# Who sums which chunks of the first modulation, and when the rotary keys are turned

## The chip, the cores and the metric

The kernel runs on one core of a Trainium2 chip. The metric is the device time of one execution in microseconds; the median of the runs counts. The core has TensorE (matmuls), VectorE, ScalarE, GpSimd and SyncE (SP), which only issues loads; 16 DMA engines serve all queues.

## What is computed

One layer over 256 tokens of width 2048. The part that matters here is its opening:

```python
ada = jnp.dot(jax.nn.silu(c), w_ada) + b_ada          # c is one row of 2048
shift1, scale1, gate1, shift2, scale2, gate2 = jnp.split(ada[:, None, :], 6, axis=-1)
h = layer_norm(x) * (1 + scale1) + shift1
z, xbc, dt_raw, q_a, kv_a, k_r, g_logits = jnp.split(jnp.dot(h, w_in), IN_OFFSETS, axis=-1)
...
q = jnp.dot(rms_norm(q_a, q_norm_w), w_uq)            # attention (MLA), 16 heads
kv = jnp.dot(rms_norm(kv_a, kv_norm_w), w_ukv)
k_pe = apply_rope(k_r, cos, sin)                      # the rotary keys, shared by all heads
```

After it come attention, a state-space branch, gates, an output projection, and a PEER layer that gathers 128 experts for each token. They are not touched by the change.

## The kernel before

The first modulation (`shift1` and `scale1`) is a product of one row with 2048 x 4096 weights, 32 MB. It is cut into four quarters of 1024 output columns (`QUARTERS`), and each quarter into eight chunks of 256 weight rows, 1 MB each: 32 chunks, numbered n = 8q + j. Five buffers in SBUF hold them (`ADA_BUFS`).

- SP loads the chunks in order (`ada1_chunk`, L521 to L531). For n >= 5 it waits until chunk n - 5 has been used, by the counter `ada_used` (VectorE) or `ada_pe_used` (TensorE). Its queue is in order: a wait holds back all that follows, among it the weights of the first projection, two units of 1 MB for each quarter (`load`, L518), and x, which is asked for after chunk 4.
- VectorE sums chunks j = 0 to 6 of a quarter into an accumulator of 128 partitions (`ada1_chunks`, L1548 and L1550): two instructions a chunk. TensorE sums chunk 7 straight into PSUM with 1-column matmuls (`ada1_rest`, L690), then adds the accumulator's sum over partitions (`ada1_sums`, L699), for which it waits for VectorE (`acc_ready`); `acc_summed` tells VectorE that a quarter's row is there.
- `h_quarter` on VectorE (L1564 to L1574) makes scale and shift from PSUM, applies them to a quarter of the turned, normalised x (`xnT`), waits for ScalarE's rounded copy (`h_hi`, L1125), subtracts it (`h_lo`) and makes the low parts of the quarter's two weight units (`wlo`, L1481), of which ScalarE has made the high parts (`whi`, L1064). TensorE then multiplies the two units (`token_unit`, L634 to L636), three matmuls for each product.
- The order on VectorE: quarter 0's chunks; copies of the parameter columns; normalising x; then for each q from 1: chunks 0 to 2 of q, all of `h_quarter(q - 1)`, chunks 3 to 6 of q. On TensorE: the turns of the parameters, which wait for 17 small loads on ScalarE's queue (`params_in`, L674); chunk 7 and sums of quarter 0; the turns of x (L713); then for each quarter its two units, after them chunk 7 and the sums of the next.

Before attention TensorE turns `dk` (dt and rotary key, L751), VectorE rotates the keys (`kpe2`, L1678 to L1684), TensorE turns them (L756), ScalarE copies them (L1168, L1169, `kpe_read`), and only then TensorE enters attention's loop of four rounds (`pe.Fori(0, 4)`). A round opens with two units of the queries (k = 0, 1: channel matmuls and rope columns), then two of keys and values. In a chunk of code after the rotated keys, VectorE computes dt (L1689 to L1700).

Of the kernel before, what the change touches and what calls it, by code (L numbers as in the profile page):

```python
# [17 lines left out]
P = 128  # L18
# [3 lines left out]
DC = D // P  # L22
# [60 lines left out]

QUARTERS, ADA_V, ADA_BUFS = 4, 7, 5

# [45 lines left out]
def build(nc, a, out, stop="all"):  # L131
    ctx = ExitStack()
    with ctx:
# [272 lines left out]
        b_free = sem("b_free")  # L406
# [101 lines left out]
        def _(sp_):  # L508
# [13 lines left out]
            def ada1_chunk(q, j):  # L522
                n = 8 * q + j
                if n >= ADA_BUFS:

                    q0, j0 = divmod(n - ADA_BUFS, 8)
                    if j0 < ADA_V:
                        sp_.wait_ge(ada_used, q0 * ADA_V + j0 + 1)
                    else:
                        sp_.wait_ge(ada_pe_used, q0 * (8 - ADA_V) + j0 - ADA_V + 1)  # L530
                sp_.dma_start(ada1_in(n), a["p_ada1"][ds(n * P, P), :]).then_inc(ada_full[n % ADA_BUFS], 16)  # L531
# [83 lines left out]
        def _(pe):  # L615
# [63 lines left out]

            ada_sum = aux[:, 3, :]  # L680

            def ada1_rest(q):

                for j in range(ADA_V, 8):
                    n = 8 * q + j
                    pe.wait_ge(ada_full[n % ADA_BUFS], 16 * (n // ADA_BUFS + 1))
                    for kc in range(2):
                        for t in range(8):
                            c = t * P
                            last = mm(ada_sum[:, 8 * q + t:8 * q + t + 1],  # L690
                                      ada1_in(n)[:, 2 * W * kc + c:2 * W * kc + c + P],
                                      csil[:, 2 * j + kc:2 * j + kc + 1], start=(j == ADA_V and kc == 0 and t == 0),
                                      stop=False, skip_group_check=True)
                    last.then_inc(ada_pe_used, 1)

            def ada1_sums(q):
                pe.wait_ge(acc_ready, q + 1)
                for t in range(8):
                    last = mm(ada_sum[:, 8 * q + t:8 * q + t + 1], ada1_acc[:, q % 2, t * P:t * P + P],  # L699
                              con[:, C_ONE:C_ONE + 1], start=False, stop=True, skip_group_check=True)  # L700
                last.then_inc(acc_summed, 1)
# [21 lines left out]
            if on("low"):  # L723
# [9 lines left out]

                for q in range(QUARTERS):
                    pe.wait_ge(h_ready, q + 1)
                    for s in range(2):
                        token_unit(U_LOW, 2 * q + s, 0, 0, h_hi, h_lo, 4 * q, DC - 1,
                                   [ps[:, s, b, :] for b in range(BLK)])
                    if q + 1 < QUARTERS:
                        ada1_rest(q + 1)  # L740
                        ada1_sums(q + 1)
# [6 lines left out]
                for k in range(2):  # L748
                    pe.wait_ge(dk_copied, k + 1)
                    for b in range(BLK):  # L750
                        last = nc.tensor.transpose(aux[:, b, 64 * k:64 * k + 64], dk[:, k, b * P:b * P + P],  # L751
                                                   ident[0:64, 0:64])
                    last.then_inc(dk_turned, 1)
                pe.wait_ge(kpe_ready, 1)
                for b in range(BLK):
                    last = nc.tensor.transpose(aux[:, 3, b * P:b * P + P],  # L756
                                               kpe2[:, b, :, :].rearrange("p a b -> p (a b)"), ident)
                last.then_inc(kpe_turned, 1)
            if on("att"):
                pe.wait_ge(cn_split, 2)  # L760
                pe.wait_ge(kpe_read, 1)
                with pe.Fori(0, 4) as i:
                    for k in range(2):
                        if k == 1:
# [4 lines left out]
                                     [(ps[:, 1, k, e * SEQ:e * SEQ + SEQ], e * QH, e == 0) for e in range(2)], used=False)  # L769
                        if k == 0:  # L770

                            pe.wait_ge(b_free, i + 1)
# [4 lines left out]
                        for b in range(BLK):  # L777
                            o = ps[:, 0, 0, b * 256 + k * P:b * 256 + k * P + P]
                            t = slice(b * P, b * P + P)
                            for kc in range(RC):  # L780
                                mm(o, cqT_hi[:, kc, t], rope[0][:, kc], start=(kc == 0), stop=False)
                                mm(o, cqT_lo[:, kc, t], rope[0][:, kc], start=False, stop=False)
                                last = mm(o, cqT_hi[:, kc, t], rope[1][:, kc], start=False, stop=(kc == RC - 1))
                        last.then_inc(pe_used, 1)
                    for k in range(2):

# [685 lines left out]
        def _(dve):  # L1472
# [63 lines left out]
            def ada1_chunks(q, first, end):  # L1536
                if first == 0:
                    dve.wait_ge(acc_summed, q + 1)
                for j in range(first, end):
# [4 lines left out]
                    for kc in range(2):  # L1544
                        k = 2 * j + kc
                        src = tile[:, 2 * W * kc:2 * W * kc + 2 * W]
                        if k == 0:
# [5 lines left out]
                    if j < ADA_V - 1:  # L1553
                        last.then_inc(ada_used, 1)
                        dve.wait_ge(ada_used, q * ADA_V + j + 1)
                    else:
                        last.then_inc(acc_ready, 1)
                        dve.wait_ge(acc_ready, q + 1)
                        dve.sem_inc(ada_used, 1)

            def h_quarter(q):

                dve.wait_ge(acc_summed, q + 3)
                link(V.tensor_tensor(adacol[:, 4 * q:4 * q + 4], aux[:, 3, 8 * q:8 * q + 4],  # L1564
                                     cols[:, PC_ADA + 4 * q:PC_ADA + 4 * q + 4], ALU.add))
                link(V.scalar_tensor_tensor(adacol[:, DC + 4 * q:DC + 4 * q + 4], aux[:, 3, 8 * q + 4:8 * q + 8], 1.0,
                                            cols[:, PC_ADA + DC + 4 * q:PC_ADA + DC + 4 * q + 4], ALU.add, ALU.add))
                dve.wait_ge(xT_ready, q + 1)
                for k in range(4 * q, 4 * q + 4):
                    last = V.tensor_scalar(xnT[:, k, :], xnT[:, k, :], adacol[:, DC + k:DC + k + 1],  # L1570
                                           adacol[:, k:k + 1], ALU.mult, ALU.add)
                    S.step(last) if k % 4 < 3 else last.then_inc(h_full, 1)
                dve.wait_ge(h_hi_ready, q + 1)
                V.tensor_tensor(h_lo[:, 4 * q:4 * q + 4, :], xnT[:, 4 * q:4 * q + 4, :],  # L1574
# [4 lines left out]
            dve.wait_ge(c_ready, 1)  # L1579
            ada1_chunks(0, 0, ADA_V)  # L1580
            dve.wait_ge(rows_turned, 1)
# [6 lines left out]
            for q in range(1, QUARTERS):  # L1588
                ada1_chunks(q, 0, 3)
                h_quarter(q - 1)  # L1590
                ada1_chunks(q, 3, ADA_V)
            h_quarter(QUARTERS - 1)

            V.memset(kpeT[64:P, 0, :], 0.0).then_inc(kpe_zero, 1)
# [683 lines left out]
```

## Time and profile before

| | us |
|---|---|
| median of 3 runs | 2896.03 (2895.16 to 2896.86) |
| profiled execution | 2899.7 |
| its span, first to last instruction | 2898.0 |
| TensorE busy | 2396.8 (83%) |
| VectorE busy | 2106.9 (73%) |
| ScalarE busy | 1002.1 (35%) |
| GpSimd busy | 882.0 (30%) |
| mean granted clock of TensorE | 0.912 |

Busy shares are means over stages that have different limits. The part that the change touches is the first 195 us or so. There VectorE, TensorE and the loads take turns in being last, so the timeline of each engine and the times at which SP issues its loads say more than the shares. PE stands for TensorE, PEld for its weight loads, DVE for VectorE, ACT for ScalarE, SPq for the issues of SP. A long matmul row "x32" holds 16 matmuls of two pieces each.

### The profile page before, as it was taken

Reading aid. Unit: us, or ns where it says so; the run is one execution under the profiler, and the core shown is the slowest. Engines: PE = TensorE matmul, PEld = TensorE weight load, DVE = VectorE, ACT = ScalarE, POOL = GpSimd, SP = SyncE. Lnnn points to the kernel's source line nnn. Section 1 sums busy time; section 2 is a strip of 40 time slices with the busy share of each in tenths; the row PEclk is TensorE's granted clock in tenths of the full one; section 3 lists DMA queues with packets and bytes.
Section 4 is the critical chain, followed back from the end, with each engine's and each line's share of the span. In section 5 each row is a group of like instructions: output and inputs, shape, how many; then the busy total and the mean of one; then the engine's idle time right before and its main releaser. Section 6 shows DMA issues by size and latency. Waiting matters only on the chain.

```text
span 2898.0 us, 38848 instructions
## 1 busy us (share of the span) xinstructions
PE 2396.8 (83%) x14598; PEld 2021.0 (70%) x14598; DVE 2106.9 (73%) x2541; ACT 1002.1 (35%) x1389; POOL 882.0 (30%) x725
## 2 busy tenths in 40 slices
PE   4589999999999999999869866665656669999990
PEld 3589998888888888999759766665655654444440
DVE  7766668777877786444574788888888896665568
ACT  1144442344444444433343222224767660000000
POOL 0000001122222221000100555756656724444343
PEclk9799999999999999999989878877777889999995
DMA  8745658766656555555544799999999949999995
GB/s 342 294 169 202 223 203 285 254 210 211 204 190 211 197 203 175 221 188 181 210 145 175 279 366 398 372 377 382 375 376 390 394 176 413 413 414 414 415 412 229
DMA packets 144961, 817.83 MB, mean 282 GB/s; under 512 B 16520, under 2 KB 21248, under 8 KB 70832
## 3 DMA queue, kind: packets, MB, share of 16 engines
q0 software_dynamic: 93200, 477.21, 42.4%
q1 hardware_dynamic: 49728, 336.05, 31.4%
q10 hardware_dynamic: 1888, 2.59, 0.2%
q8 instruction: 97, 1.59, 0.2%
q14 instruction: 48, 0.39, 0.0%
HBM read 811.55 MB, written 4.23 MB: 281 GB/s over the span
## 4 chain that ended last, share of the span: by engine, by line
PE 41%; DVE 23%; DMA 21%; issue 8%; POOL 3%; ACT 3%; ACTq 0%; DVEq 0%; POOLq 0%
DMA vrow<-in_p_vg,acc 12%; PE ps L654 9%; PE ps L656 9%; PE ps L655 9%; DMA rrow<-in_peer_u,acc 7%; DVE rrow L2030 4%; DVE ps L2059 3%; POOL rrow L2198 3%; DVE wlo L1481 2%; DVE acc L1530 2%; ACT whi L1064 2%; PE ps L634 2%; PE ps L635 2%; PE ps L636 2%; DVE oh L2072 1%
## 5 line engine op out<-in xcount | busy, mean ns | idle before, releaser
L1481 DVE TENSOR_TENSOR wlo<-raw,whi 128x2048 fp32r<-128x2048 f32 x216 | 504.8, 2339 | 376.6 <-ACT whi L1064 366.6
L1064 ACT ACTIVATE whi<-raw 128x2048 fp32r<-128x2048 f32 x216 | 412.8, 1913 | 707.1 <-PE ps L656 486.2
L2198 POOL DMA_INDIRECT rrow<-in_peer_u,acc x256 | 443.5, 1733 | 455.8 <-DVE acc L1978 202.3
L2030 DVE CUSTOM_DVE_ANT_0 rrow<-rrow,h 128x2048 f32<-128x2048 f32 x200 | 450.0, 2290 | 61.1 <-DMA rrow<-in_peer_u,acc 60.8
L654 PE MATMUL ps<-h_hi,whi 128*128 128x256 f32 (+1 forms) x1568 | 454.9, 290 | 9.3 <-issue 5.7
L2059 DVE SCALAR_TENSOR_TENSOR ps<-vrow,acc,ps 128x1024 f32<-128x1024 f32 x254 | 327.2, 1288 | 167.8 <-DMA vrow<-in_p_vg,acc 154.1
L1049 PE MATMUL aux<-vden,wt 128*128 128x512 f32 x1024 | 441.7, 594 | 4.7 <-DMA vden<-in_p_vd 4.0
L655 PE MATMUL ps<-h_lo,whi 128*128 128x256 f32 (+1 forms) x1568 | 445.1, 284 | 0.0
L656 PE MATMUL ps<-h_hi,wlo 128*128 128x256 f32 (+1 forms) x1568 | 445.0, 284 | 0.0
L1049 PEld LDWEIGHTS aux<-vden,wt 128*128 128x128 f32 x1024 | 195.0, 191 | 250.8 <-issue 245.1
L2198 POOL DMA_INDIRECT vrow<-in_p_vg,acc x256 | 247.4, 966 | 305.6 <-DVE ps L2059 220.0
L654 PEld LDWEIGHTS ps<-h_hi,whi 128*128 128x128 f32 (+1 forms) x1568 | 300.7, 192 | 22.0 <-issue 14.0
L655 PEld LDWEIGHTS ps<-h_lo,whi 128*128 128x128 f32 (+1 forms) x1568 | 300.9, 192 | 4.0 <-issue 3.8
L656 PEld LDWEIGHTS ps<-h_hi,wlo 128*128 128x128 f32 (+1 forms) x1568 | 300.7, 192 | 0.0
L2128 POOL DMA_DIRECT2D ada_in<-in_p_ada x128 | 69.3, 542 | 751.1 <-DVEq L1631 602.1
L994 PE MATMUL ps<-con,rrow 128*128 128x128 f32 x896 | 174.1, 375 | 142.5 <-DMA rrow<-in_peer_u,acc 141.6
L994 PEld LDWEIGHTS ps<-con,rrow 128*128 128x128 f32 x896 | 157.5, 200 | 151.6 <-DMA rrow<-in_peer_u,acc 150.4
L1004 PE MATMUL aux<-hT,rT 128*128 128x128 f32 x1792 | 229.8, 290 | 5.3 <-ACT rT L1382 5.2
L1004 PEld LDWEIGHTS aux<-hT,rT 128*128 128x128 f32 x1792 | 226.4, 208 | 9.4 <-ACT rT L1382 8.8
L1530 DVE SCALAR_TENSOR_TENSOR acc<-ada_in,csil,acc 128x512 f32<-128x512 f32 x240 | 202.3, 843 | 28.5 <-DMA ada_in<-in_p_ada 15.2
L1382 ACT ACTIVATE rT<-ps 128x1024 f32<-128x1024 f32 x112 | 113.0, 1023 | 289.8 <-PE ps L994 289.7
L1079 ACT ACTIVATE st<-st,con 128x2 f32<-128x2 f32 (+1 forms) x18 | 5.2, 294 | 507.6 <-DVE st L1508 507.3
(331 smaller groups left out, 4165.6 us busy)
## 6 DMA issues: line engine op xcount, KB each, us to landing
raw<-in_p_in SPq DMA_DIRECT2D x104, 1024.0 KB, 4.9
ada_in<-in_p_ada POOLq DMA_DIRECT2D x128, 512.0 KB, 5.2
vden<-in_p_vd SPq DMA_DIRECT2D x64, 1024.0 KB, 8.0
ada_in<-in_p_ada SPq DMA_DIRECT2D x32, 1024.0 KB, 9.7
raw<-in_p_so SPq DMA_DIRECT2D x32, 1024.0 KB, 4.8
raw<-in_p_mo SPq DMA_DIRECT2D x16, 1024.0 KB, 7.1
raw<-in_p_bc SPq DMA_DIRECT2D x16, 1024.0 KB, 4.9
raw<-in_p_mix SPq DMA_DIRECT2D x16, 1024.0 KB, 4.8
```

The lines of the kernel that those rows point to most:

```text
L654: mm(o, wh, x_hi[:, k, :], start=(k == 0 and first), stop=False, skip_group_check=True)
L655: mm(o, wh, x_lo[:, k, :], start=False, stop=False, skip_group_check=True)
L656: last = mm(o, wl, x_hi[:, k, :], start=False, stop=(k == klast), skip_group_check=True)
L994: last = nc.tensor.transpose(ps[:, half, t // 4, (t % 4) * P:(t % 4) * P + P], rrow[:, r % ROWS, c:c + P], ident)
L1004: last = mm(aux[:, 3, j * P:j * P + P], rT[:, kc, :], hT[b][:, kc, :], start=(kc == 0), stop=(kc == DC - 1), skip_group_check=True)
L1049: last = mm(aux[:, 2 * b + n, :], wt[b][:, 2 * u + q, :], vden[u % 4][:, q, n * W:n * W + W], start=(u == 0 and q == 0), stop=(u == NVU - ...
L1064: F(whi[:, n % 2, :, 0:cols_], raw[:, n % 4, :, 0:cols_], ACT.Copy).then_inc(hi_ready, 1)
L1481: V.tensor_tensor(wlo[:, n % 2, :, 0:cols_], raw[:, n % 4, :, 0:cols_], whi[:, n % 2, :, 0:cols_].bitcast(F32), ALU.subtract).then_inc(lo_ ...
L1530: last = V.scalar_tensor_tensor(acc_, tile[:, kc, :], csil[:, k:k + 1], acc_, ALU.mult, ALU.add)
L2030: last = V.tensor_tensor_reduce(row, row, h2[:, b, :], 1.0, 0.0, ALU.mult, ALU.add, dots[:, k, e:e + 1])
L2059: last = V.scalar_tensor_tensor(o, row, w, o, ALU.mult, ALU.add)
L2198: return G.indirect_dma_start(out=dst, out_offset=None, in_=table, in_offset=bass.IndirectOffsetOnAxis(ap=eid_all[:, r:r + 1], axis=0))
```

## The change

Four things are changed.

1. VectorE sums six chunks of a quarter instead of seven (`ADA_V` 7 to 6), TensorE two (`ADA_PE`): chunks 0 and 1 instead of chunk 7. SP's waits follow: before chunk n is loaded, n - 5 with j of 0 or 1 must have been used by TensorE, the others by VectorE. This holds for quarter 0 too.
2. On TensorE `ada1_rest(q + 1)` stands ahead of the wait for `h_ready` and of quarter q's units, instead of behind them. The sums of odd quarters go to another PSUM bank, `aux[:, 2]`.
3. On VectorE `h_quarter` is cut in two. Its second part, `h_low`, stands one chunk later: chunk 2 of q, `h_quarter(q - 1)`, chunk 3, `h_low(q - 1)`, chunks 4 to 7.
4. The turn of the rotary keys becomes `turn_kpe`, called behind the first unit (i = 0, k = 0) of attention; the waits for `cn_split` 2, `kpe_read` and (for i = 0) `b_free` move behind the second unit. TensorE's loop over the four rounds is written out (`for i in range(4)`), the other engines keep theirs.

```diff
-QUARTERS, ADA_V, ADA_BUFS = 4, 7, 5
+QUARTERS, ADA_V, ADA_BUFS = 4, 6, 5
+ADA_PE = 8 - ADA_V
...
-                    if j0 < ADA_V:
-                        sp_.wait_ge(ada_used, q0 * ADA_V + j0 + 1)
+                    if j0 < ADA_PE:
+                        sp_.wait_ge(ada_pe_used, q0 * ADA_PE + j0 + 1)
                     else:
-                        sp_.wait_ge(ada_pe_used, q0 * (8 - ADA_V) + j0 - ADA_V + 1)
+                        sp_.wait_ge(ada_used, q0 * ADA_V + j0 - ADA_PE + 1)
...
-            ada_sum = aux[:, 3, :]
+            def ada_sum(q):
+
+                return aux[:, 3 - q % 2, :]
...
-                for j in range(ADA_V, 8):
+                for j in range(ADA_PE):
...
                 for q in range(QUARTERS):
+                    if q + 1 < QUARTERS:
+                        ada1_rest(q + 1)
                     pe.wait_ge(h_ready, q + 1)
                     for s in range(2):
                         token_unit(U_LOW, 2 * q + s, 0, 0, h_hi, h_lo, 4 * q, DC - 1,
                                    [ps[:, s, b, :] for b in range(BLK)])
                     if q + 1 < QUARTERS:
-                        ada1_rest(q + 1)
                         ada1_sums(q + 1)
...
+            def turn_kpe():
                 pe.wait_ge(kpe_ready, 1)
...
             if on("att"):
-                pe.wait_ge(cn_split, 2)
-                pe.wait_ge(kpe_read, 1)
-                with pe.Fori(0, 4) as i:
+                for i in range(4):
...
-                        if k == 0:
+                        if k == 0 and i:
 
                             pe.wait_ge(b_free, i + 1)
...
+                        if (i, k) == (0, 0):
+                            turn_kpe()
+                    if i == 0:
+
+                        pe.wait_ge(b_free, 1)
+                        pe.wait_ge(cn_split, 2)
+                        pe.wait_ge(kpe_read, 1)
...
-            ada1_chunks(0, 0, ADA_V)
+            ada1_chunks(0, ADA_PE, 8)
...
             for q in range(1, QUARTERS):
-                ada1_chunks(q, 0, 3)
+                ada1_chunks(q, ADA_PE, 3)
                 h_quarter(q - 1)
-                ada1_chunks(q, 3, ADA_V)
+                ada1_chunks(q, 3, 4)
+                h_low(q - 1)
+                ada1_chunks(q, 4, 8)
             h_quarter(QUARTERS - 1)
+            h_low(QUARTERS - 1)
```

## Rows read from the trace of the kernel before

**Rows 1.** The chain of waits, 0 to 230 us: start, duration, what.
```profile
9.11 24.99 DMA dskip<-in_D_skip
...
96.12 11.07 DMA ada_in<-in_p_ada
...
133.27 3.46 PE aux L690 x32
```

**Rows 2.** Windows: length, PE, PEld, DVE, ACT, POOL busy (count), PEclk, DMA share, GB/s.
```profile
243.00:248.00 5.00, 5.00 (x46) 5.00 (x45) 0.51 (x1) 2.68 (x4) 0.00 (x0) 1.00 0.76 284
```

**Rows 3.** Timeline of TensorE, first matmuls of quarters 0 and 3 (of four).
```profile
59.51 0.77 PE L634 MATMUL ps<-whi,h_hi 128*128 128x512 f32 x1 [8.32 <-DVE wlo L1481]
...
145.70 0.77 PE L634 MATMUL ps<-whi,h_hi 128*128 128x512 f32 x1 [7.18 <-DVE wlo L1481]
```

**Rows 4.** SP's issues (sixth chunk), and from issue to landing of all 32.
```profile
13.20 0.33 SPq L531 DMA_DIRECT2D ada_in<-in_p_ada  x1
...
DMA to landing us min/median/max: 4.7/9.7/17.7
```

**Rows 5.** Timeline of TensorE and its weight loads: modulation chunks, sums, turns of x.
```profile
35.22 6.83 PE L690 MATMUL aux<-csil,ada_in 128*128 128x1 f32 x32
41.91 3.55 PE L699 MATMUL aux<-con,ada_acc 128*128 128x1 f32 x16
45.32 5.86 PE L713 MATMUL ps<-con,x_in 128*128 128x128 f32 x32
...
49.63 0.99 PEld L713 LDWEIGHTS ps<-con,x_in 128*128 128x128 f32 x8
...
72.31 3.62 PE L690 MATMUL aux<-csil,ada_in 128*128 128x1 f32 x32
...
105.79 1.93 PE L699 MATMUL aux<-con,ada_acc 128*128 128x1 f32 x16
```

**Rows 6.** Timeline of VectorE: normalising x, chunks of the modulation.
```profile
35.82 2.46 DVE L1503 BATCH_NORM_STATS2 acc<-x_in 128x6 f32<-128x512 f32 x4
...
61.48 10.53 DVE L1550 SCALAR_TENSOR_TENSOR ada_acc<-ada_in,csil,ada_acc 128x1024 f32<-128x1024 f32 x8
72.23 0.75 DVE L1548 TENSOR_SCALAR ada_acc<-ada_in,csil 128x1024 f32<-128x1024 f32 x1 [0.22 <-DVE ada_acc L1550]
```

**Rows 7.** A window in which the loads run without a break.
```profile
100.00:105.00 5.00, 5.00 (x36) 4.57 (x35) 3.37 (x4) 0.00 (x0) 0.00 (x0) 1.00 1.01 424
```

**Rows 8.** DMA queues (packets, MB, share of 16 engines): 20 to 25 us; 23 to 35 us.
```profile
q1 hardware_dynamic: 272, 1.99, 97.9%
q10 hardware_dynamic: 272, 0.01, 3.7%
...
q10 hardware_dynamic: 544, 0.10, 4.4%
```

**Rows 9.** Timeline of VectorE, `h_lo` behind ScalarE's `h_hi` (one of four).
```profile
84.64 1.22 DVE L1574 TENSOR_TENSOR h_lo<-xnT,h_hi 128x1024 fp32r<-128x1024 f32 x1 [1.12 <-ACT h_hi L1125]
```

**Rows 10.** Timeline of TensorE before attention and in its first round.
```profile
172.82 0.34 PE L751 MATMUL aux<-con,dk 64*128 64x64 f32 x2 [1.64 <-ACT dk L1160]
178.80 0.69 PE L756 MATMUL aux<-con,kpe 128*128 128x128 f32 x2 [5.64 <-DVE kpe L1684]
180.64 0.57 PE L654 MATMUL ps<-cqT_hi,whi 128*128 128x256 f32 x1 [1.15 <-ACT kpeT L1169]
...
194.28 0.33 PE L654 MATMUL aux<-ckT_hi,whi 128*128 128x256 f32 x1
```

**Rows 11.** Timeline of VectorE and of ScalarE (last row), the same stretch.
```profile
168.28 2.29 DVE L1481 TENSOR_TENSOR wlo<-raw,whi 128x2048 fp32r<-128x2048 f32 x1 [0.61 <-ACT whi L1064]
...
178.53 0.22 DVE L1684 TENSOR_TENSOR kpe<-krs,krt 128x64 f32<-128x64 f32 x1
...
184.02 0.29 DVE L1700 SCALAR_TENSOR_TENSOR adt<-dtv,anegA 128x128 f32<-128x128 f32 x1
...
188.93 1.92 ACT L1064 ACTIVATE whi<-raw 128x2048 fp32r<-128x2048 f32 x1 [7.34 <-PE ps L783]
```

More of the change, by code:

```diff
@@ L689, in ada1_rest @@
                             c = t * P
-                            last = mm(ada_sum[:, 8 * q + t:8 * q + t + 1],
+                            last = mm(ada_sum(q)[:, 8 * q + t:8 * q + t + 1],
                                       ada1_in(n)[:, 2 * W * kc + c:2 * W * kc + c + P],
-                                      csil[:, 2 * j + kc:2 * j + kc + 1], start=(j == ADA_V and kc == 0 and t == 0),
+                                      csil[:, 2 * j + kc:2 * j + kc + 1], start=(j == 0 and kc == 0 and t == 0),
                                       stop=False, skip_group_check=True)
@@ L698, in ada1_sums @@
                 for t in range(8):
-                    last = mm(ada_sum[:, 8 * q + t:8 * q + t + 1], ada1_acc[:, q % 2, t * P:t * P + P],
+                    last = mm(ada_sum(q)[:, 8 * q + t:8 * q + t + 1], ada1_acc[:, q % 2, t * P:t * P + P],
                               con[:, C_ONE:C_ONE + 1], start=False, stop=True, skip_group_check=True)
@@ L1536, in ada1_chunks @@
             def ada1_chunks(q, first, end):
-                if first == 0:
+                if first == ADA_PE:
                     dve.wait_ge(acc_summed, q + 1)
@@ L1546, in ada1_chunks @@
                         src = tile[:, 2 * W * kc:2 * W * kc + 2 * W]
-                        if k == 0:
+                        if k == 2 * ADA_PE:
                             last = V.tensor_scalar(acc_, src, csil[:, k:k + 1], None, ALU.mult)
@@ L1552, in ada1_chunks @@
                             link(last)
-                    if j < ADA_V - 1:
+                    if j < 7:
                         last.then_inc(ada_used, 1)
-                        dve.wait_ge(ada_used, q * ADA_V + j + 1)
+                        dve.wait_ge(ada_used, q * ADA_V + j - ADA_PE + 1)
                     else:
@@ L1563, in h_quarter @@
                 dve.wait_ge(acc_summed, q + 3)
-                link(V.tensor_tensor(adacol[:, 4 * q:4 * q + 4], aux[:, 3, 8 * q:8 * q + 4],
+                link(V.tensor_tensor(adacol[:, 4 * q:4 * q + 4], aux[:, 3 - q % 2, 8 * q:8 * q + 4],
                                      cols[:, PC_ADA + 4 * q:PC_ADA + 4 * q + 4], ALU.add))
-                link(V.scalar_tensor_tensor(adacol[:, DC + 4 * q:DC + 4 * q + 4], aux[:, 3, 8 * q + 4:8 * q + 8], 1.0,
+                link(V.scalar_tensor_tensor(adacol[:, DC + 4 * q:DC + 4 * q + 4], aux[:, 3 - q % 2, 8 * q + 4:8 * q + 8], 1.0,
                                             cols[:, PC_ADA + DC + 4 * q:PC_ADA + DC + 4 * q + 4], ALU.add, ALU.add))
@@ L1572, in h_quarter, with h_low @@
                     S.step(last) if k % 4 < 3 else last.then_inc(h_full, 1)
+            def h_low(q):
                 dve.wait_ge(h_hi_ready, q + 1)
```

## The prediction

> **What bounds the kernel now.** I read the chain of waits first, for the part that the diff touches, the first 195 us. It gives each stretch to what ended last [rows 1]: until 34.1 us the last small parameter load on ScalarE's queue (24.99 us), then VectorE, a weight chunk's transfer twice (the longer 11.07 us), at the end of the third quarter TensorE's own chunk of the modulation (3.46 us), and before attention the turned rotary keys. So no engine bounds this part alone: it is a ring of VectorE, TensorE and SP's load queue, in which five buffers decide when the next chunk may be asked for. From 195 us on TensorE is busy 5.00 of 5.00 us in each window that I read, up to 253 us (one of them in [rows 2]), so I take what the front part gains or loses as passed on to the end one for one.
>
> The marks by which I count are the first units of the four quarters: TensorE starts them at 59.5, 88.9, 119.7 and 145.7 us, each after a wait for `wlo` (8.3 us the first, 7.2 the last) [rows 3]. The third stage of reading is the start: SP asks for the sixth chunk (n = 5) at 13.20 us, as soon as VectorE has used chunk 0 [rows 4]. TensorE first sums at 35.2 us, since it stands behind the parameter loads [rows 5].
>
> **Prices.** VectorE: eight instructions take 10.53 us, 1.32 each, so 2.64 us a chunk (0.75 + 1.32 = 2.07 for a quarter's first); normalising x runs from 35.82 until TensorE may turn it, 9.3 us [rows 5, 6]. TensorE, one chunk: 6.69 us at 1.2 GHz (35.22 to 41.91), 3.5 at 2.4 GHz (3.62 in the row, the next starts after 3.49); the eight sums 3.4 or 1.93 us; turning x 5.9 us [rows 5]. Two units: 59.5 to 72.3, 12.8 us [rows 3, 5], up to 13.4 (88.9 to 102.3) where they begin with the low clock. A chunk's transfer: 4.7 us from issue to landing on an idle queue [rows 4], 2.5 us behind others (1.05 MB at 424 GB/s, the DMA engines busy throughout) [rows 7].
>
> **Part 1: TensorE takes chunks 0 and 1 instead of 7.** VectorE loses one chunk a quarter, 4 x 2.64 = 10.6 us of its own work. But at the start this turns against the kernel. The buffers of chunks 0 and 1 are now freed by TensorE, whose order is unchanged: parameters first. SP's wait for n = 5 holds back everything behind it in its queue (chunks 5, 6, 7, the first units' weights, all later chunks), and VectorE waits for chunks 5 to 7 before it normalises x.
>
> When do the parameters land? SP's queue then runs dry near 23 us: 0.48 MB of constants and seven transfers of 1.05 MB, at about 400 GB/s. Until 35 us the small queue q10 gets one packet for each of q1 (272 and 272 in 20 to 25 us); 544 packets are still to come at 23 us [rows 8], 34 for each of the 16 engines. The floor is their own time (544 packets took 4.4% of 16 x 12 us, 16 ns each, so 0.5 us: 23.5 us). The ceiling is the landing of before, 34.1. The nearest row is the landing on an idle queue, which is 2.2 us over its transfer: 23 + 0.5 + 2.2, so I take 26.
>
> From there, step by step. TensorE turns the parameters (1.1 us) and sums chunk 0 until 33.8 and chunk 1 until 40.5, at the low clock as before. n = 5 is asked for at 33.8 and lands at 38.5; n = 6 at 40.5 and 45.2; n = 7 lands at 47.7, then chunk 8, two units and chunk 9 until 57.7. VectorE ends chunk 5 at 41.2, 6 at 47.9, 7 at 50.5, copies the columns (0.9) and has x normalised at 60.7, against 45.1. TensorE turns x until 66.8. So far 15.6 us are lost.
>
> Now `ada1_rest(1)` stands ahead of the first units: chunk 8 from 66.8 at the high clock (turning x raised it before, too: its last pieces follow at 0.12 us, the mean is 0.18 [rows 5]) 3.5 us, chunk 9 mostly at the low clock, 5.3 us. The units start at 75.6 (VectorE would be ready at 73.3, since ScalarE copies the turned x until 67.9, 7.2 us behind the start of the turns as before). That is 16.1 us late. Chunk 8's buffer is freed at 70.3, 9's at 75.6, so SP's queue has idled again since 65.2; n = 13 lands at 75.0, 14 at 80.3, then one each 2.5 us, with two units among them: n = 18 at 95.3. Units 0 and 1 end at 88.7, the sums at 90.7.
>
> Second quarter: chunk 18 until 97.4, `h_quarter(1)` 1.8, chunk 19 2.6 us (it hides ScalarE's 1.1 us of `h_hi`, on which VectorE waited before [rows 9]), then `h_lo` and the first `wlo` 3.5: the units start at 105.5, +16.6. VectorE ends chunk 23 at 118.2, the units end at 118.9, the sums at 120.8, chunks 24 and 25 at the low clock at 131.1. Third: chunk 26 until 122.8, modulation, chunk 27, `wlo` until 130.8: units at 131.1, +11.4. This is where VectorE's shorter list pays. Fourth: VectorE ends chunk 31 at 143.6, units end at 144.5 and nothing of TensorE's own stands between them and the sums (3.5 us before), which end at 146.4 against 138.5. The units follow 7.2 us behind as before: 153.6 against 145.7. Part 1: **+7.9 us**.
>
> Here the Trainium skill speaks, for the change. "TensorE: Matmul & The Clock Gate", Part 1 on the clock gate, has the clock follow how busy TensorE is, and makes no exception for narrow matmuls. By that rule chunks 0 and 1 would run up to the high clock, and the sum would be near the fast rival's below. The trace disagrees: from 35.0 to 45.4 us TensorE is busy throughout and the pieces of 1-column matmuls still follow at 0.21 us and more [rows 5].
>
> **Part 2: turned keys behind the opening unit.** Before, TensorE ended the `dk` turns at 173.15, waited 5.6 us for `kpe`, turned it (0.7), waited 1.15 for ScalarE's copy and began unit 0 at 180.64, much of it at the low clock; unit 1 from 188.8 [rows 11], unit 2 at 194.3 [rows 10]. Unit 0's weights were ready at 170.6 [rows 11]. In before's times: unit 0 from 173.2 at the high clock, 5.5 us as unit 1 (188.8 to 194.3), to 178.7; keys ready at 178.75 [rows 11], turned by 179.2; unit 1 to 184.7. ScalarE copies the keys by 180.0 and makes `whi` of unit 2 in 1.9 us [rows 11], ahead of 184.3 even with the table load between; VectorE ends its `dt` chain at 184.3 [rows 11] and `wlo` at 186.6. Unit 2 starts at 186.7, 7.6 us earlier; the moved waits (`b_free`, `cn_split`, `kpe_read`) are met by then. If unit 0 ran at the low clock: 8.2 us instead of 5.5, a gain of 4.9. I take **-7.6 us**. The written-out loop costs nothing that I can see: TensorE is busy 5.00 of 5.00 us where the loop turns (243 to 248 us) [rows 2], and if each of three turns had hidden 0.3 us (an issue on SP's queue, the nearest small price [rows 4]), it would be 1 us either way.
>
> **Sum.** The profiled execution took 2899.7 us, 1.7 around its span; +7.9 - 7.6 = +0.3 gives 2900.0. The median of the runs is 3.7 lower, so the forecast is **2896.3 us**. A measurement here can tell about 0.2%, 5.8 us.
>
> **Rivals.** (a) Slower: the parameters land late. The mechanism is the start of part 1 alone; each microsecond past 26 goes through TensorE's chunks 0 and 1 to the buffers and to every later mark. It decides from 31.6 us; at 34.1 the time is 2904.4. For it: in before only the last third of q10's packets took 11 us. Against it: in that time each waited for a packet of q1, which is gone. Chunks 8 and 9 both at the low clock (+4.6 for 80.2 instead of 75.6) would bring it nearer. Chance 0.22, with the case that unit 0 in attention runs at the low clock.
> (b) Faster: the clock rises in the sums. If chunks 0 and 1 were at the high clock after 4 us, they would take 4 + 1.4 x 3.49 = 8.9 instead of 13.4 us, and chunk 9 3.5 instead of 5.3: 6.3 us, so 2890.0. Against it stand the 10 us above. Chance 0.06.
> (c) Faster: the start costs less than I think, since a later stage takes it up. VectorE's saving is 10.6 us in all, of which my schedule uses about 8; if loads never idled, the 27 chunks and 8 unit loads from 33.8 on would be in at 33.8 + 4.7 + 34 x 2.5 = 123.5, not 138.3. With half of that regained (7 us) the time is 2889. Chance 0.09.
> (d) The change does nothing of part 2, because unit 0 meets another wait: 2903.9. Nothing in rows 10 and 11 speaks for it. Chance 0.04.
> My forecast has 0.59. The range of 2889.5 to 2904.5 reaches to (a) and (b). Faster 0.14, within 0.2% 0.61, slower 0.25 (the rest of (a) and (d)).
>
> **What would show it.** In the new profile: the first modulation chunk on TensorE near 27 us; n = 5 asked for near 34 instead of 13.2 us; an idle stretch of DMA from 23 to 34 us; x normalised near 61; first units at 75.6, 105.5, 131.1 and 153.6; after the `dk` turns no wait of 5.6 us; unit 2 of attention some 41 us behind the fourth quarter's units instead of 48.6. The forecast is wrong if n = 5 is asked for before 30 or after 38 us, if the chunks' pace on TensorE is not 6.7 us at the start, or if attention does not pass the shift on.

## The result, and the profile after

| | before | after |
|---|---|---|
| median, us | 2898.21 | 2906.87 |
| profiled execution, us | 2899.7 | 2904.0 |
| its span, us | 2898.0 | 2902.3 |
| TensorE busy, us | 2396.8 | 2416.9 |
| VectorE busy, us | 2106.9 | 2095.1 |
| mean granted clock | 0.912 | 0.917 |

The kernel became slower: the ratio is 1.0028, interval 1.0020 to 1.0037, which on 2898.2 is +8.1 us, +5.8 to +10.7. The forecast was 2896.3 us with a range up to 2904.5, so the result lies outside it. Of the 10.6 us between 2896.3 and 2906.87, 2.2 are the base: the forecast stood on a median of 2896.03 from 3 runs of the kernel before, and 11 runs have 2898.21. VectorE did lose 11.8 us of work (10.6 forecast); TensorE gained 20.1 us. Neither says anything of the end: the marks do.

The timeline of TensorE after, from the parameters to the units of the fourth quarter (start, duration; L694 is a modulation chunk, L703 the sums, L717 the turns of x, L636 the first matmul of a quarter's units; x64 is two chunks):

```profile
24.43 0.86 PE L676 MATMUL aux<-con,rows 120*128 120x120 f32 x3 [19.59 <-DMA dskip<-in_D_skip]
25.51 13.65 PE L694 MATMUL aux<-csil,ada_in 128*128 128x1 f32 x64
49.67 3.57 PE L703 MATMUL aux<-con,ada_acc 128*128 128x1 f32 x16 [10.51 <-DVE ada_acc L1562]
...
59.84 5.88 PE L717 MATMUL ps<-con,x_in 128*128 128x128 f32 x32 [6.60 <-DVE x_in L1527]
65.56 8.76 PE L694 MATMUL aux<-csil,ada_in 128*128 128x1 f32 x64
74.18 0.77 PE L636 MATMUL ps<-whi,h_hi 128*128 128x512 f32 x1
...
88.54 11.32 PE L694 MATMUL aux<-csil,ada_in 128*128 128x1 f32 x64
105.41 0.77 PE L636 MATMUL ps<-whi,h_hi 128*128 128x512 f32 x1 [5.55 <-DVE wlo L1493]
119.76 11.65 PE L694 MATMUL aux<-csil,ada_in 128*128 128x1 f32 x64
131.27 0.77 PE L636 MATMUL ps<-whi,h_hi 128*128 128x512 f32 x1
...
153.41 0.77 PE L636 MATMUL ps<-whi,h_hi 128*128 128x512 f32 x1 [7.17 <-DVE wlo L1493]
```

Read against [rows 3, 5]: the sums of quarter 0, at 41.91 before, are at 49.67 now, since TensorE waits 10.51 us for VectorE; x is turned 14.5 us later; the four quarters' units start 14.7, 16.5, 11.6 and 7.7 us later than before (before's middle ones were at 88.9 and 119.7).

The clock of the first two chunks has to be read from their pace. The windows show a granted clock of 1.00 there (columns as in [rows 2]), but the trace's first record of the clock stands at 64.1 us (at 49.8 in the kernel before), so the column says nothing about the time ahead of it:

```profile
25.50:39.00 13.50, 13.50 (x66) 13.50 (x64) 1.60 (x2) 0.46 (x1) 0.00 (x0) 1.00 0.23 78
```

A piece takes 0.21 us in the row at 25.51, as in quarter 0 before (6.83 us for 32) and against 3.62 us for 32 in a row with the clock recorded at 2.4 GHz [rows 5]. By that pace the two chunks ran at 1.2 GHz, and so did chunk 7 before.

Why the start is late stands in SP's timeline, VectorE's, and the DMA totals from 24 to 32 us:

```profile
32.37 8.11 SPq L533 DMA_DIRECT2D ada_in<-in_p_ada  x4
...
37.36 2.61 DVE L1562 SCALAR_TENSOR_TENSOR ada_acc<-ada_in,csil,ada_acc 128x1024 f32<-128x1024 f32 x2 [16.42 <-DMA ada_in<-in_p_ada]
44.37 5.25 DVE L1562 SCALAR_TENSOR_TENSOR ada_acc<-ada_in,csil,ada_acc 128x1024 f32<-128x1024 f32 x4 [4.40 <-DMA ada_in<-in_p_ada]
...
DMA packets 0, 0.00 MB, mean 0 GB/s; under 512 B 0, under 2 KB 0, under 8 KB 0
```

n = 5 is asked for at 32.37 instead of 13.20 us [rows 4], after TensorE's chunk 0. For 8 us not a byte is loaded, and VectorE stands idle for 16.42 and 4.40 us.

What SP's queue waited for in all between 44 and 160 us, first before, then after (total, times, longest):

```profile
SPq L531 <- DVE ada_acc L1550: 49.4, 13, 11.4
...
SPq L531 <- PE aux L690: 7.7, 2, 4.2
```
```profile
SPq L533 <- PE aux L694: 50.9, 6, 19.2
SPq L533 <- DVE ada_acc L1562: 21.2, 7, 6.9
```

The buffers are now held back mainly by TensorE: 50.9 us of waiting where there were 7.7.

Attention's beginning, TensorE and one row of VectorE (L756 `dk`, L762 the keys, L656 a unit, L1493 `wlo`):

```profile
180.44 0.34 PE L756 MATMUL aux<-con,dk 64*128 64x64 f32 x2 [1.64 <-ACT dk L1172]
180.70 0.39 PE L656 MATMUL ps<-cqT_hi,whi 128*128 128x256 f32 x1
...
186.42 0.44 PE L762 MATMUL aux<-con,kpe 128*128 128x128 f32 x2
...
191.84 2.28 DVE L1493 TENSOR_TENSOR wlo<-raw,whi 128x2048 fp32r<-128x2048 f32 x1
...
194.27 0.55 PE L656 MATMUL aux<-ckT_hi,whi 128*128 128x256 f32 x1 [1.92 <-DVE wlo L1493]
```

The wait of 5.6 us of [rows 10] is gone: unit 0 follows the `dk` turns at once. From there to the third unit it is 13.83 us instead of 21.46. The third unit starts at 194.27 us, as before it (194.28), though its quarter's units had been 7.7 us late. But now TensorE waits 1.92 us for VectorE, whose `dt` chain stands ahead of `wlo`, and loses its clock. Windows of 2 us (columns as in [rows 2]), before, then after:

```profile
194.00:196.00 2.00, 2.00 (x18) 2.00 (x18) 0.00 (x0) 1.52 (x1) 0.00 (x0) 1.00 0.68 197
```
```profile
192.00:194.00 2.00, 0.36 (x4) 0.21 (x2) 2.00 (x1) 1.61 (x1) 0.00 (x0) 0.95 0.00 1
194.00:196.00 2.00, 1.73 (x8) 1.76 (x9) 1.79 (x2) 1.39 (x3) 0.00 (x0) 0.50 0.44 70
196.00:198.00 2.00, 2.00 (x14) 2.00 (x14) 2.00 (x5) 0.00 (x0) 0.00 (x0) 0.69 0.92 389
```

That fall costs 1.3 us: the unit behind the `probs` matmuls (L832, L844 after) starts at 409.93 us before and at 411.19 after, and the third units had started at 194.28 and 194.27.

### The profile page after: what moved, and what is told of

Its sections match the earlier page's. It is cut to its first block, busy times and chain, and to the rows that moved or that the text cites. A ratio compares the mean times of both kernels' runs of the same rounds, so it can differ in the third digit from the quotient of the medians.

```text
span 2902.3 us, 39040 instructions
## 1 busy us (share of the span) xinstructions
PE 2416.9 (83%) x14726; PEld 2040.5 (70%) x14726; DVE 2095.1 (72%) x2533; ACT 1001.8 (35%) x1389; POOL 884.4 (30%) x725
## 4 chain that ended last, share of the span: by engine, by line
PE 41%; DVE 22%; DMA 21%; issue 9%; POOL 3%; ACT 3%; DVEq 0%; ACTq 0%; POOLq 0%
DMA vrow<-in_p_vg,acc 12%; PE ps L656 9%; PE ps L658 9%; PE ps L657 9%; DMA rrow<-in_peer_u,acc 7%; DVE rrow L2047 3%; DVE ps L2076 3%; POOL rrow L2215 3%; DVE wlo L1493 2%; DVE acc L1542 2%; PE ps L636 2%; PE ps L637 2%; PE ps L638 2%; ACT whi L1076 2%; DVE oh L2089 1%
## 5 line engine op out<-in xcount | busy, mean ns | idle before, releaser
L1493 DVE TENSOR_TENSOR wlo<-raw,whi 128x2048 fp32r<-128x2048 f32 x216 | 503.5, 2332 | 372.6 <-ACT whi L1076 353.4
L656 PE MATMUL ps<-h_hi,whi 128*128 128x256 f32 (+1 forms) x1568 | 453.8, 289 | 9.0 <-DVE wlo L1493 5.0
L656 PEld LDWEIGHTS ps<-h_hi,whi 128*128 128x128 f32 (+1 forms) x1568 | 299.6, 191 | 21.9 <-issue 11.0
L1006 PEld LDWEIGHTS ps<-con,rrow 128*128 128x128 f32 x896 | 155.4, 198 | 157.5 <-DMA rrow<-in_peer_u,acc 156.5
## 6 DMA issues: line engine op xcount, KB each, us to landing
ada_in<-in_p_ada SPq DMA_DIRECT2D x32, 1024.0 KB, 11.6
```

The source lines that it names most:

```text
L656: mm(o, wh, x_hi[:, k, :], start=(k == 0 and first), stop=False, skip_group_check=True)
L1006: last = nc.tensor.transpose(ps[:, half, t // 4, (t % 4) * P:(t % 4) * P + P], rrow[:, r % ROWS, c:c + P], ident)
L1493: V.tensor_tensor(wlo[:, n % 2, :, 0:cols_], raw[:, n % 4, :, 0:cols_], whi[:, n % 2, :, 0:cols_].bitcast(F32), ALU.subtract).then_inc(lo_ ...
```

## The experiments

Times are medians; ratios stand against the kernel before on the same chip. The column "units" has the starts of the fourth quarter's units and of attention's third unit in the profiled execution; the last column is from that third unit to the end of the span.

| kernel | median | ratio, interval | units | to the end |
|---|---|---|---|---|
| before | 2898.2 | | 145.7, 194.3 | 2703.7 |
| after | 2906.9 | 1.0028, 1.0020 to 1.0037 | 153.4, 194.3 | 2708.0 |
| `p1_only` | 2913.9 | 1.0056, 1.0043 to 1.0069 | 156.5, 205.3 | 2711.0 |
| `p2_only` | 2891.4 | 0.9981, 0.9970 to 0.9993 | 146.7, 187.7 | 2701.2 |
| `loop_only` | 2898.1 | 0.9998, 0.9989 to 1.0008 | 146.1, 194.6 | 2704.2 |
| `q0_old` | 2889.5 | 0.9972, 0.9962 to 0.9982 | 142.3, 183.7 | 2705.9 |
| `after_again` | 2908.1 | 1.0035, 1.0022 to 1.0048 | 156.0, 198.7 | 2706.1 |
| `sums_first` | 2894.4 | 0.9987, 0.9977 to 0.9996 | 144.4, 187.2 | 2712.2 |
| `q01_old` | 2890.0 | 0.9974, 0.9964 to 0.9983 | 148.2, 189.3 | 2708.2 |
| `q012_old` | 2891.4 | 0.9976, 0.9967 to 0.9984 | 141.1, 183.8 | 2705.9 |
| `v6_behind` | 2924.2 | 1.0090, 1.0077 to 1.0103 | 162.7, 211.9 | 2710.2 |
| `dt_later` | 2891.2 | 0.9979, 0.9970 to 0.9987 | 144.8, 185.0 | 2709.8 |
| `fill` | 2913.0 | 1.0054, 1.0036 to 1.0071 | 157.0, 199.5 | 2712.9 |

### The parts by themselves

`p1_only` is points 1 to 3 of the change; `p2_only` is point 4; `loop_only` only writes out TensorE's loop.

```diff
-                with pe.Fori(0, 4) as i:        # loop_only
+                for i in range(4):
```

> Part 1 alone: the chunks of the first modulation as in the changed kernel, attention's opening and its loop as in the kernel before. Theory A (the two parts add, and the downstream only wobbles with the low clock): units of the four quarters start near 74, 105, 131 and 153.4 us as in the changed kernel, attention's third unit at 194.3 + 7.6 = 201.9 us, and the time is 7 to 8 us above the kernel before. Theory B (the part of the loss that the marks of the front do not show, 4 to 7 us, belongs to part 1, through what comes after attention): 12 to 15 us above. Theory C (that part belongs to the written-out loop): 7 to 8 us, as A; the next two runs tell A from C.

> Part 2 alone: turned keys behind attention's first unit, moved waits, TensorE's loop written out; the modulation as before. Theory A: attention's third unit starts at 194.3 - 7.6 + 1.3 = 188.0 us at the worst clock (as in the changed kernel, where TensorE stood 1.9 us before it and fell to the low clock), and the time is 6 to 7.6 us below the kernel before. Theory C (the written-out loop costs 4 us or more later): only 1 to 3 us below.

> The kernel before with TensorE's loop over attention's four rounds written out, nothing else. Theory A: no difference (within 1.5 us). Theory C (longer code has to be fetched, and that costs time in attention or behind it): 4 us or more above the kernel before, with TensorE's rows in attention later than before from the second round on.

Against the before of the same chip (2897.57) part 1 costs 16.2 us (12.5 to 20.0), part 2 gives back 5.5 (2.0 to 8.7), and the loop nothing (-3.2 to +2.3). 16.2 - 5.5 = 10.7 is near the whole change's 8.1, so the parts add within their intervals. `p1_only` is slower than theory A had it (7 to 8 us) and nearer to B (12 to 15): its third unit is 11.0 us late, not 7.6, and more is lost behind it. `p2_only` is nearer to A (6 to 7.6) than to C (1 to 3). In `p1_only` the wait for the keys stands as before; in `p2_only` the third unit meets the same wait as in after:

```profile
189.74 0.69 PE L761 MATMUL aux<-con,kpe 128*128 128x128 f32 x2 [5.65 <-DVE kpe L1694]
```
```profile
187.74 0.55 PE L654 MATMUL aux<-ckT_hi,whi 128*128 128x256 f32 x1 [1.92 <-DVE wlo L1488]
```

### Which piece of part 1 costs

`q0_old` is after with quarter 0 divided as before (TensorE: chunk 7). `sums_first` is after with TensorE's chunks 0 and 1 ahead of its wait for the parameters; `after_again` is after on that chip.

```diff
+def pe_chunks(q):                                     # q0_old
+    return (7,) if q == 0 else tuple(range(ADA_PE))
...
-                for j in range(ADA_PE):
+                for j in pe_chunks(q):
...
-            pe.wait_ge(params_in, 16 * 17)                    # sums_first, with the turns behind it
...
             ada1_rest(0)
+            pe.wait_ge(params_in, 16 * 17)
...
             ada1_sums(0)
```

> The changed kernel, but quarter 0 keeps its old division: VectorE sums chunks 0 to 6, TensorE chunk 7; quarters 1 to 3 as in the changed kernel. Theory D (the whole loss of part 1 is the start, where the buffers of chunks 0 and 1 wait for TensorE behind the parameter loads): the sixth chunk is asked for at 13.2 us again, x is normalised at 45.1, units start near 60.3, 87, 113 and 136 us, 15 to 18 us ahead of the changed kernel in the end, so the time is 12 to 18 us below the kernel before. Rival E (the new order of quarters 1 to 3 has a loss of its own, TensorE's two chunks at the low clock ahead of the units): the gain over the changed kernel is under 10 us and the time within 4 us of the kernel before.

> The changed kernel once more, for a second profiled execution. Theory F (the first one fell well: TensorE's chunks 8 and 9 took 8.8 us there, against 11.6 us in the kernel with part 1 alone, because the clock fell later): this time they take 10.5 to 11.7 us, the first units start near 77 instead of 74.2 us, the fourth quarter's near 156 instead of 153.4, attention's third unit 2 to 3 us later than 194.3, and the profiled time is 2 to 4 us above the first one's 2904.0. Rival G (the median's 3 us over the first profile come from the stages behind attention only): chunks 8 and 9 take 8.8 us again and the marks up to attention's third unit are those of the first profile within 1 us.

> The changed kernel with TensorE's two chunks of quarter 0 ahead of its wait for the parameter loads and their turns. Theory D2 (the start's loss is the wait behind the parameters, not the new division): chunk 0 is summed from 11.4 us on, the sixth chunk is asked for near 18 us and the seventh near 25, VectorE ends chunk 7 near 35 us and x is normalised near 45.5, as in the kernel before; from there it runs as the kernel with quarter 0 divided as before, units near 62.8, 94, 119.5 and 142.3 us, and the time is 6 to 11 us below the kernel before. Rival: two chunks at TensorE's low clock (13.4 us) are the loss by themselves; then x is normalised 5 us or more later than 45.1 and the time is within 3 us of the kernel before.

Moving one wait, and the turns of the parameters with it, behind two chunks is worth 13.8 us (2908.14 to 2894.38), dividing quarter 0 as before 17.4 (2906.87 to 2889.49, on two chips; 16.2 by the ratios). The start of part 1 is its loss, and as `sums_first` shows it is the place behind the parameters, not the division. TensorE in `sums_first`:

```profile
11.17 13.81 PE L686 MATMUL aux<-csil,ada_in 128*128 128x1 f32 x64 [6.12 <-ACT csil L1124]
27.18 0.86 PE L703 MATMUL aux<-con,rows 120*128 120x120 f32 x3 [2.20 <-DMA dskip<-in_D_skip]
...
45.66 6.46 PE L717 MATMUL ps<-con,x_in 128*128 128x128 f32 x32 [6.60 <-DVE x_in L1527]
```

x is turned at 45.66, as before it (45.32), against 59.84, and n = 5 is asked for at 18.2 us: the marks of theory D2. The times fall short of the theories, though. `sums_first` is 3.8 us below the kernel before (1.2 to 6.7), where D2 had 6 to 11; `q0_old` 8.1 us below (5.2 to 11.0), between D (12 to 18) and E (within 4), with its fourth quarter's units at 142.3 where D had 136. `p2_only`, without any of part 1, has 2891.4: `q0_old` is 2 us better (2.6 by the ratios), `sums_first` not at all. So the new order of quarters 1 to 3, with VectorE relieved of three chunks (7.9 us of work), brings at most 2 or 3 us, which the intervals can't tell from nothing. `after_again` met theory F in the late marks (156.0, 198.7, the profile 2.6 us above the first) but not in the cause it gave: chunks 8 and 9 took 9.4 us and the first units came at 74.3, while the next pair took 13.3. TensorE and VectorE of `q0_old` show two costs that stand against the gain:

```profile
51.41 11.48 PE L705 MATMUL aux<-csil,ada_in 128*128 128x1 f32 x64
...
84.06 0.75 DVE L1572 TENSOR_SCALAR ada_acc<-ada_in,csil 128x1024 f32<-128x1024 f32 x1 [10.94 <-DMA ada_in<-in_p_ada]
```

TensorE's two chunks now take 11.48 us ahead of the first units, which start at 62.7 instead of 59.5, and hold two of five buffers for so long; VectorE waits 10.94 us for chunk 18.

### How many quarters, and in which order

`q01_old` leaves quarters 0 and 1 as before, `q012_old` all but the last. `v6_behind` is before with `ADA_V` 6: TensorE sums two chunks, 6 and 7, behind the units.

```diff
-    return (7,) if q == 0 else tuple(range(ADA_PE))   # q01_old: q < 2; q012_old: q < 3
...
-QUARTERS, ADA_V, ADA_BUFS = 4, 7, 5                   # v6_behind
+QUARTERS, ADA_V, ADA_BUFS = 4, 6, 5
```

> Quarters 0 and 1 divided and ordered as in the kernel before (TensorE sums chunk 7 behind the units), quarters 2 and 3 as in the changed kernel (chunks 0 and 1 ahead of the units). Theory H (the new order pays only where TensorE waits for `wlo` anyway; ahead of the first units it does not wait, and its two chunks at 10.5 us or so put them back and hold two buffers): first units at 59.5 to 60, second near 89, third near 116, fourth near 139 us against 142.3 with quarter 0 alone as before, and the time is 9 to 13 us below the kernel before. Rival: holding the buffers of chunks 16, 17, 24 and 25 costs as much in any quarter; then the fourth quarter's units start no earlier than 142 us and the time is 6 to 8 us below, as with quarter 0 alone.

> Quarters 0, 1 and 2 divided as in the kernel before, only the last quarter as in the changed kernel. Theory H: third units near 119, the last quarter's near 140 to 142 us (before: 145.7; TensorE's 3.5 us of chunk 31 no longer stand between its units and the sums), and the time is 8 to 11 us below the kernel before. Rival: no gain of the new division in any quarter; then the fourth units start at 145 us or later and the time is 5.5 us below, as with the turned keys alone.

> The kernel before with one number changed: VectorE sums six chunks of each quarter, TensorE chunks 6 and 7, both behind the quarter's units and ahead of the sums, as chunk 7 was. It tells the count from the place. The start loses nothing (the sixth chunk is asked for at 13.2 us, x normalised near 45 us), but TensorE's order is now 13.4 us of units, 7 to 10.5 us of chunks, 1.9 of sums, and VectorE's modulation and first `wlo` of 7.2 to 10 us behind it. Expected: units near 60, 92, 124 and 155 us, attention's third unit near 203, the time 8 to 12 us above the kernel before. Rival (VectorE is the limit, so a shorter list helps in any place): fourth units before 143 us and the time below the kernel before.

The three kernels that keep quarter 0 are alike (2889.5, 2890.0, 2891.4), so what the new order wins is won by any one quarter of it or hardly at all. Theory H missed for `q01_old`: 7.5 us below the kernel before, not 9 to 13, the second quarter's units at 95.8 and the fourth's at 148.2 (its profiled execution was 9.2 us above its median, so these marks are late ones). `q012_old` met H's marks (119.4 and 141.1) and not quite its time, 7.0 us below (4.6 to 9.6) for 8 to 11. `v6_behind` missed on the slow side by some 15 us (+26.9 us). The start did lose, against what was expected: chunks 6 and 7 put 13.65 us ahead of the turns of x, which began at 52.3. And in the fourth quarter VectorE has nothing to do while TensorE sums:

```profile
143.16 8.97 PE L690 MATMUL aux<-csil,ada_in 128*128 128x1 f32 x64
...
155.57 0.16 DVE L1564 TENSOR_TENSOR adacol<-aux,cols 128x4 f32<-128x4 f32 x1 [15.76 <-PE aux L699]
```

From the turns of x to the fourth quarter's units it needs 110.5 us, before 100.4, after 93.6, `sums_first` 98.8, each from one execution. So, given two chunks on TensorE, the order of the change is worth some 12 to 17 us over the old one. What it doesn't do is beat one chunk by much.

### The new wait in attention

`dt_later` is `q012_old` with VectorE's `dt` chain moved into attention's first round, behind the keys and values and the first rows of the second modulation.

> The kernel with quarters 0 to 2 divided as before and the turned keys behind attention's first unit, and one thing more: VectorE's chain for dt (5.6 us, ahead of `wlo` of attention's third unit) moved into the first round, behind the first rows of the second modulation; VectorE's loop written out for that. Theory K (the 1.9 us that TensorE waits before its third unit, and the low clock behind it, 1.3 us, come from that chain): the wait shrinks to 1 us or less, where ScalarE's `whi` is next in line, the clock stays high, and the time is 2 to 3 us below the same kernel without it, so 7 to 10 us below the kernel before. Rival: the chain is then late for the scores of round 0; the wait only moves, and the time is that of the same kernel without it or above.

The chain is gone from in front of the third unit, and TensorE still waits 0.99 us for `wlo` there (`q012_old`: 1.01); the clock fell behind both waits. VectorE's `wlo` in `q012_old`, then in `dt_later`:

```profile
181.35 2.29 DVE L1506 TENSOR_TENSOR wlo<-raw,whi 128x2048 fp32r<-128x2048 f32 x1 [0.35 <-ACT whi L1089]
```
```profile
182.52 2.29 DVE L1506 TENSOR_TENSOR wlo<-raw,whi 128x2048 fp32r<-128x2048 f32 x1 [4.56 <-ACT whi L1089]
```

In both it starts when ScalarE's `whi` is there; in that execution of `q012_old` the chain was not what ended last. From the `dk` turns to the third unit it takes 12.9 us instead of 14.3, but these 1.4 us are unit 0's: it ran at 2.4 GHz in `dt_later` (granted 1.00, the keys turned 5.98 us behind `dk`) and partly at 1.2 in `q012_old` (0.50 at 172:174 us, 7.36). Against the kernels whose unit 0 was as fast (`after`, `q01_old`, `p2_only`: 13.8 us, with waits of 1.9) the move wins 0.9 us. The median is that of `q012_old` (2891.2 and 2891.4): theory K's wait came down to 1 us, its gain of 2 to 3 us is not confirmed.

### TensorE's clock in the two chunks

In after's executions the pairs of chunks took 8.8, 11.3 and 11.6 us; in later ones 9.4, 13.3, 10.6 (`after_again`), 11.3, 10.9, 10.9 (`after_third`) and 8.6, 11.1, 11.3 (`after_fourth`). The difference is when the clock falls. After, then `after_third`:

```profile
68.00:70.00 2.00, 2.00 (x20) 2.00 (x19) 1.50 (x2) 2.00 (x2) 0.00 (x0) 1.00 0.00 0
```
```profile
65.80 11.33 PE L694 MATMUL aux<-csil,ada_in 128*128 128x1 f32 x64
...
68.00:70.00 2.00, 2.00 (x13) 2.00 (x13) 1.39 (x2) 2.00 (x3) 0.00 (x0) 0.59 0.00 0
```

Behind the same work, in the same window, one is still at 2.4 GHz and the other mostly at 1.2. `fill` puts a turn of 128 columns of x behind every second 1-column matmul, to hold the clock.

```diff
+                            if q and t % 2 == 0:
+                                nc.tensor.transpose(aux[:, 0, 0:P], x_in[:, 0, 0:P], ident)
```

> The change, and in quarters 1 to 3 TensorE also turns a 128x128 block of x (a result nobody reads) behind every second 1-column matmul of its two chunks, 16 turns in 32 matmuls; the turns of x ran at the high clock. Theory L (the clock falls because 1-column matmuls follow each other alone): the pair of chunks stays at the high clock for all or most of its length, some 7 us plus 16 turns of 0.09 to 0.18 us = 8.5 to 10 us instead of 11.3 (mean of after's later executions) and every time alike; the fourth quarter's units some 1.5 to 3 us earlier than 156.5, the median 2 to 5 us below that of after. Rival M (the turns are too few to hold the clock): the pair takes 11.3 us plus 16 turns of 0.18 to 0.36, 14 to 17 us, and the time is 6 to 15 us above after.

```profile
66.00:70.00 4.00, 4.00 (x41) 4.00 (x41) 2.82 (x3) 4.00 (x4) 0.00 (x0) 1.00 0.00 0
70.00:74.00 4.00, 4.00 (x24) 4.00 (x23) 4.00 (x3) 0.92 (x1) 0.00 (x0) 0.52 0.79 262
```

The clock fell at about 70 us all the same; the pairs took 10.9, 12.7 and 13.4 us with the turns, and the median is 6.2 us above after's. Theory L is wrong as put; rival M was right in kind, though the turns cost less than it said. Whether denser wide work would hold the clock was not tried.

### What lies behind attention's third unit

> The kernel before once more, for a second profiled execution. Question: from attention's third unit to the end the profiles took 2703.7 us (before), 2704.2 (loop written out) and 2701.2 (turned keys alone), but 2705.9 to 2712.2 us in the seven kernels with some of part 1. Theory I (these stretches scatter by a few us in any kernel, since the clock falls at other places): this time it lies anywhere in 2701 to 2710. Theory J (part 1 costs some 4 us behind attention, though nothing there was edited): 2701 to 2705 again.

> The changed kernel once more, for a third profiled execution (the first two: third unit of attention at 194.3 and 198.7 us, from there to the end 2708.0 and 2706.1 us). Theory F2 (TensorE's pair of chunks at the low or the high clock moves the front by 3 to 4 us from execution to execution): third unit of attention at 194 to 199 us. Theory J: from there to the end 2705 us or more; theory I: anything from 2701 to 2710.

> The kernel before, unchanged. From attention's third unit to the end of the span it had 2703.7 and 2703.8 us in two executions. Theory J (the 4 us behind that unit belong to the kernels with part 1): 2703 to 2705. Theory I (scatter of one execution): up to 2708 is possible.

> The kernel after, unchanged. From attention's third unit to the end it had 2708.0, 2706.1 and 2707.8 us. Theory J: 2706 to 2709. Theory I: 2703 to 2705 is as likely. Its fourth quarter's units start between 153.4 and 156.8 us, by how long TensorE's pairs of chunks stay at the low clock.

> Part 2 alone, unchanged. From attention's third unit to the end its one execution had 2701.2 us, the shortest of all. Theory J (part 2 takes nothing away behind that unit): 2703 to 2705, the first look was scatter. Rival: again 2701 to 2702, so that part 2 wins 2 us more behind the unit.

| | fourth quarter's units | third unit | from there to the end |
|---|---|---|---|
| before, `before_again`, `before_fourth` | 145.7, 144.9, 145.5 | 194.3, 193.6, 194.3 | 2703.7, 2703.8, 2699.2 |
| after, `after_again`, `after_third`, `after_fourth` | 153.4, 156.0, 156.8, 153.1 | 194.3, 198.7, 198.1, 194.1 | 2708.0, 2706.1, 2707.8, 2708.6 |
| `p2_only`, `p2_again` | 146.7, 145.7 | 187.7, 188.3 | 2701.2, 2706.0 |

The stretch behind the third unit scatters by up to 5 us between executions of one kernel, so single readings prove nothing (theory I). Yet of the twelve executions in which TensorE sums two chunks in some quarter none is under 2705.9 us (mean 2708.9), while the six of kernels without that, `loop_only`'s 2704.2 among them, have a mean of 2703.0 and only one above 2704.2, `p2_again` with 2706.0. Some profiled executions are poor samples of their kernel (`q01_old` 9.2, `sums_first` 6.7, `dt_later` 5.4 and `p1_only` 4.2 us above the median), but after's four lie by 5.4 us in the mean above before's three. A difference is likely (theory J), its size uncertain, and `p2_only`'s 2701.2 was scatter. Compared at the same matmuls, counted from the end, the mean of after less that of before is +1.0 us in the first 34 us behind the third unit (the clock, above), +3.4 from 378 to 941 us behind it, where the executions of before alone differ by 4.0, +1.1 from 1360 to 2372 us (they differ by 3.0), and 0.1 or less elsewhere. In the stretch of +3.4 the three executions without part 1 but with the loop written out have 563.2 to 564.2 us, before 559.6 to 563.6, after 563.7 to 566.3, so in that stretch after's mean lies only 1 us above theirs. No mechanism was found: some 4 us remain open.

## Why the prediction was wrong

The forecast named the right bounds and, in the first profiled execution, met the marks. The parameters landed at 24.4 us (26), n = 5 was asked for at 32.4 (33.8), x was normalised at 59.8 (60.7), and the units came at 74.2, 105.4, 131.3 and 153.4 (75.6, 105.5, 131.1, 153.6); the third unit at 194.3 (194.6). Point by point:

- **Part 1, +7.9 us to the fourth quarter's units.** +7.7 in the first execution; over all, 154.8 against 145.4 in the mean, +9.4. The terms that are too small are the pairs of chunks ahead of the units: 3.5 + 5.3 us for chunks 8 and 9 held in two executions of four (8.8 and 8.6), in the others it was 9.4 and 11.3; chunks 24 and 25, for which I had 10.3, took 10.6 to 11.6. I took where the clock falls from one execution, as if it were fixed. That the first execution agreed to 0.2 us was luck.
- **Part 2, -7.6 us.** From the `dk` turns to the third unit the first executions differ by 7.63 us (21.46 to 13.83). But before's others took 20.49 and 20.51, after's 14.28, 13.84 and 13.84, so the mean gain is 6.9. Unit 0 ran at the high clock in three executions of four; in `after_again` the clock fell within it (granted 0.50 at 186:188 us) and the keys were turned 7.37 us behind `dk` instead of 5.98. I had seen that VectorE's `wlo` would end last ahead of the third unit, but gave the wait no price of its own: in the other three the clock fell behind it, +1.3 us or more, 1.0 in the mean of the four. Together this term is 5.9, near the 5.5 of `p2_only`.
- **The loop, nothing:** shown by `loop_only`.
- **"Passed on to the end one for one": this step failed.** Mean of the executions in the last table: at the third unit after stands at 196.3 against 194.1, +2.2 us where I had +0.3; at the end of the span it is +7.7. The 1.9 us too little at the third unit are the sizes of the two parts, above. Of the 5.4 us behind it, 1.0 are the clock in attention; the other 4.4 are measured but not explained, and that cause stays open. The reason that I gave, TensorE busy in the windows that I read, covers 195 to 253 us and says nothing about the 2600 us behind.
- **Rivals.** (a) had the direction (slower, 0.22 with the clock cases), but not the way: the parameters landed early, and chunks 8 and 9 took 9.5 us in the mean, 0.7 more than forecast where (a) had 4.6. What lies behind attention no rival had. (b) is refuted in quarter 0: 13.65 us at 0.21 us a piece. Here the Trainium skill, "TensorE: Matmul & The Clock Gate", Part 1 on the clock gate, has the clock follow how busy TensorE is; the trace disagrees, for TensorE is busy throughout that row and its pace stays that of 1.2 GHz. (c) is refuted: with half of the loss regained the fourth quarter's units would have been 1 us late, and they were 7.7 to 11.5 us later than before's mean. (d) is refuted by `p2_only`.

One more thing the steps hid: I counted the 8.2 us that quarters 1 to 3 make up (16.1 late, then 7.9) as the relief of VectorE. `sums_first`, with the start on time, has its fourth quarter's units only 1.3 us ahead of before, `q0_old` 3.4 (one execution each). So I take most of what is made up as slack that a late start leaves in the ring, not gain; no run shows this by itself.

## What to carry to other kernels

Before work that frees a buffer is given to another engine, see what stands ahead of it in that engine's queue: here one wait for small loads in front of two chunks cost 13.8 us, and moving it was a small edit. Work taken off the engine that looks busiest pays only where that engine ends last: 7.9 us less for VectorE was worth 2 or 3 at most. A price that hangs on TensorE's clock needs both its values in the sum: a pair of chunks took 8.6 to 13.3 us in four executions of one kernel, chunks 8 and 9 alone 8.6 to 11.3. And two kernels compared in one execution each can differ by the clock alone, as the 1.4 us between `q012_old` and `dt_later` did.

## What the hardware showed that I had not expected

- The clock falls under narrow work by itself: in unbroken 1-column matmuls behind wide ones it went from 2.4 to 1.2 GHz, between 68.3 and 70.9 us in after's four executions, and 128-column turns between them did not stop it (`fill`).
- Short waits cost the clock: one of 1.92 us was followed by some 3 us at 1.2 GHz. So were those of about 1.0 us in `q012_old`, `dt_later`, `sums_first`, `fill` and `p2_again`, but not that of 1.00 us at the same place in `after_again` (granted 1.00 from 194 to 202 us).
- With SP's queue dry the last parameter load ended by 24.4 us instead of 34.1 [rows 1]. The Trainium skill, "DMA: Bandwidth & Descriptors", Queues, rings and completion order, has each DMA engine take turns between its queues, packet by packet. The trace of before agrees: 272 packets of each of the two queues in 5 us, 1.99 MB on one and 0.01 MB on the other [rows 8]. I read it so that the queue of tiny packets waits for its neighbour's large ones.
